# Moving attention work between the input projections, and a layer norm onto GpSimd, in a fused encoder block

## The reference, cut to what matters

```
h = rms_norm(x);  proj = h @ W_in                 # [q_down 256 | kv_down 128 | k_rope 32 | conv 1024 | gates 2048]
q = rms_norm(q_down) @ w_uq                       # 8 heads x 96
k_nope, v = split(rms_norm(kv_down) @ w_ukv)      # 8 heads x 64, 8 heads x 64
q, k = rope(rms_norm(q)), rope(rms_norm([k_nope, k_rope]))
attn = chunk_causal_attention(q, k, v)            # query tiles of 128; tile j sees keys 0 .. 128*(j+1)
u = depthwise_conv31(c_val * sigmoid(c_gate))     # 512 channels
u = silu(layer_norm(u));  gates = sigmoid(gate_logits + b)
x = x + W_out(gates_A * (attn @ w_o) + gates_B * (u @ w_conv_out))
x = x + moe(rms_norm(x))                          # routing and experts: not touched
```

## Time and profile before

| | us |
|---|---|
| median of 3 runs (lowest, highest) | 1282.66 (1280.54, 1284.18) |
| the profiled execution: its time | 1281.88 |
| its span, first to last instruction | 1279.8 |
| first matmul of the input units | 70.9 |
| first matmul of the branch units | 621.09 |
| first matmul with W_out | 710.35 |
| PE busy in the span | 1182.0 (92%) |
| DVE, ACT, POOL busy | 752.9, 468.1, 198.6 |

### The profile page before, as it was taken

One profiled execution on the slowest core, in us unless ns is written; L12 is line 12 of the kernel. 1 busy time (PEld: TensorE's weight loads), 2 busy tenths in 40 slices (PEclk: granted clock), 3 DMA queues, 4 the chain that ended last, 5 costly groups with the idle time before them and its releaser, 6 DMA issues.

```text
span 1279.8 us, 14988 instructions
## 1 busy us (share of the span) xinstructions
PE 1182.0 (92%) x5452; PEld 901.6 (70%) x5452; DVE 752.9 (59%) x992; ACT 468.1 (37%) x635; POOL 198.6 (16%) x243
## 2 busy tenths in 40 slices
PE   5999999999968999999899899949999989989996
PEld 5988888887645667767788788847666656666663
DVE  3338999993424455444466434476777556656673
ACT  4432111113443444444232211124555544554552
POOL 4010000000142232220000000011222221222221
PEclk8999999999969999999799899958999999999998
DMA  6011111110100000001320233494999999999980
GB/s 224 1 50 50 49 49 50 49 49 17 42 0 1 1 1 1 1 1 34 133 81 17 79 124 115 168 323 164 327 345 311 314 318 323 341 331 308 319 270 8
DMA packets 101542, 172.28 MB, mean 135 GB/s; under 512 B 11727, under 2 KB 45690, under 8 KB 101498
## 3 DMA queue, kind: packets, MB, share of 16 engines
q1 hardware_dynamic: 91002, 154.86, 35.6%
q0 software_dynamic: 10432, 16.81, 5.4%
q10 hardware_dynamic: 64, 0.02, 0.0%
HBM read 165.35 MB, written 27.26 MB: 151 GB/s over the span
## 4 chain that ended last, share of the span: by engine, by line
PE 68%; DMA 10%; SPq 5%; DVE 5%; issue 4%; ACT 4%; POOL 2%; ACTq 0%; DVEq 0%; POOLq 0%
PE pb L1223 14%; PE pb L1224 14%; PE pb L1225 14%; DMA wgu_raw<-in_w_e_up 9%; PE pb L1505 5%; PE pb L1363 4%; PE pb L1340 4%; SPq L418 2%; PE pb L1352 2%; PE pb L1272 2%; PE pb L1477 2%; PE pb L1282 1%; SPq L415 1%; SPq L414 1%; PE pb L1423 1%
## 5 line engine op out<-in xcount | busy, mean ns | idle before, releaser
L1165 DVE TENSOR_TENSOR wgu_lo<-wgu_raw,wgu_hi 128x2048 fp32r<-128x2048 f32 x72 | 164.5, 2286 | 60.0 <-ACT wgu_hi L772 59.9
L772 ACT ACTIVATE wgu_hi<-wgu_raw 128x2048 fp32r<-128x2048 f32 x72 | 137.1, 1907 | 53.0 <-DMA wgu_raw<-in_w_e_up 52.9
L873 DVE SCALAR_TENSOR_TENSOR cv<-up,dwc,cv 128x1024 f32<-128x1024 f32 x120 | 154.1, 1284 | 3.7
L1223 PE MATMUL pb<-hT_hi,ws_hi 128*128 128x512 f32 x384 | 151.7, 395 | 0.0
L1225 PE MATMUL pb<-hT_hi,ws_lo 128*128 128x512 f32 x384 | 149.5, 389 | 0.0
L1224 PE MATMUL pb<-hT_lo,ws_hi 128*128 128x512 f32 x384 | 149.5, 389 | 0.0
L1223 PE MATMUL pb<-wgu_hi,hgT_hi 128*128 128x512 f32 x288 | 128.6, 447 | 4.3 <-DVE hgT_lo L1172 4.3
L1505 PE MATMUL pb<-wed,midT 128*128 128x512 f32 x288 | 131.2, 599 | 0.5 <-DVE midT L1198 0.5
L1225 PE MATMUL pb<-wgu_hi,hgT_lo 128*128 128x512 f32 x288 | 114.3, 397 | 0.0
L1224 PE MATMUL pb<-wgu_lo,hgT_hi 128*128 128x512 f32 x288 | 113.9, 395 | 0.0
L1505 PEld LDWEIGHTS pb<-wed,midT 128*128 128x128 f32 x288 | 54.9, 191 | 56.4 <-issue 52.9
(11 more groups left out here) (281 smaller groups left out, 2028.8 us busy)
## 6 DMA issues: line engine op xcount, KB each, us to landing
wgu_raw<-in_w_e_gate SPq DMA_DIRECT2D x36, 1024.0 KB, 11.1
wgu_raw<-in_w_e_up SPq DMA_DIRECT2D x36, 1024.0 KB, 20.2
wed<-in_w_e_down SPq DMA_DIRECT2D x36, 1024.0 KB, 18.2
ws_raw<-in_w_in SPq DMA_DIRECT2D x24, 512.0 KB, 3.8
xs<-in_x SPq DMA_DIRECT2D x8, 512.0 KB, 8.6
...
```

Of the source, the lines that this page charges most:

```text
L772: a.activation(wgu_hi[q % 2][:, :, ks, :], wgu_raw[q % SLOTS][:, :, ks, :], ACT.Copy).then_inc(gu_hi, 1)
L873: i = v.scalar_tensor_tensor(out=cv[:, c, :], in0=src, scalar=w, in1=cv[:, c, :], op0=ALU.mult, op1=ALU.add)
L1165: v.tensor_tensor(wgu_lo[q % SLOTS][:, :, ks, :], wgu_raw[q % SLOTS][:, :, ks, :], wgu_hi[q % 2][:, :, ks, :].bitcast(F32), ALU.subtract). ...
L1223: t_.matmul(out, w(0), m(0), start=start, stop=False)
```

## The change

1. **Preparation moves up.** The nine pieces of all eight tiles are placed between the matmul steps of units 1 to 16, a tile to two units, at the steps `PREP_STEP` (32 steps to a pair). They use two PSUM banks in turn (6, 7). ACT now also copies qdT (as three activations, instead of one DVE instruction) and kT, and squares in PSUM; DVE only sums. SP stores q, k and v of each tile to DRAM and loads them back (`store_prep`, `load_q`, `load_k`, `load_v`), because their SBUF is not free yet. POOL's instructions for q and k stay the same but for one short one each.
2. **Heads of tiles 0 to 3 move up**, one to every three steps, from unit 17 to 23 (`HEAD0`, `PER_HEAD`, `MIXED` = 32). There ACT makes the copy of the transposed probabilities (`probs_early`), where DVE made it. Tiles 4 to 7 follow as a loop of their own.
3. **Taps**: 6 in a unit instead of 7, spread over the steps; DVE's part of each engine's stream follows the steps. The weights' lo half is made at step 6.
4. **Layer norm** goes into tiles 4 to 7: POOL adds the four channel groups, subtracts, squares, sums, multiplies, and splits the result into `aT`; PE needs 4 matmuls in place of 16; ACT copies the mean, takes the root (head 49) and runs Silu (heads 57, 59); DVE adds eps and takes the reciprocal in four parts (heads 50 to 53).
5. **Attention output** is transposed (`attn_T`) in heads 33 to 36, 42, 50 and 58, and split straight from PSUM by ACT and DVE (`attn_lo`). The last tile's follows the first half of branch unit 0.
6. **Gates** go through DRAM: one store a unit, 16 loads beside the branch units. The rotary angles and their sine come ahead of unit 0's eviction instead of after unit 1. `EARLY` is heads 44 and 45.

```diff
@@ -57,9 +57,10 @@
...
-TAPS_PER_UNIT = 7
+TAPS_PER_UNIT = 6
+STEPS = 2 * KD
...
-LN_UNIT = 20
+MIXED = 4 * 8
...
-        at_stage = {s: i for i, s in enumerate(order)}
...
+        PREP = ("qdT", "q0", "q1", "kv0", "kv1", "qT0", "qT1", "kT0", "kT1")
+        PREP_STEP = (0, 2, 5, 8, 11, 22, 24, 29, 31)
+        PREP_UNIT = 1
+        SUMS_LATE, LO_STEP = 4, 6
+        prep_at = {STEPS * PREP_UNIT + 2 * STEPS * t + g: (k, t) for t in range(NTILE) for k, g in zip(PREP, PREP_STEP)}
...
+        HEAD0, PER_HEAD = STEPS * 17 + 8, 3
+        scores_at = {HEAD0 - 10: 0, HEAD0 - 7: 1, HEAD0 + PER_HEAD * MIXED + 1: MIXED, HEAD0 + PER_HEAD * MIXED + 5: MIXED + 1}
+        scores_at.update({HEAD0 + PER_HEAD * n: n + 2 for n in range(MIXED - 2)})
+        probs_at = {HEAD0 + PER_HEAD * n: n for n in range(MIXED)}
+        pv_at = {HEAD0 + PER_HEAD * n + 2: n for n in range(MIXED)}
+        attn_T_at = {MIXED + 1: 0, MIXED + 2: 1, MIXED + 3: 2, MIXED + 4: 3, 42: 4, 50: 5, 58: 6}
...
+        MEAN_AT, VAR_AT, SQRT_AT, RECIP_AT, SILU_AT = (37, 38), (47, 48), 49, (50, 51, 52, 53), (57, 59)
...
+            def store_prep(u):
+                t, late = divmod(u - PREP_UNIT, 2)
+                if not 0 <= t < NTILE:
+                    return
+                if late:
+                    prep_freed(("qT0", t), ("qT1", t))
+                    sp.dma_start(qT_d[t], qst[0:QK, :]).then_inc(q_out, 16)
+                    prep_freed(("kT0", t), ("kT1", t))
+                    sp.dma_start(kT_d[t], kst[0:QK, :]).then_inc(k_out, 16)
+                else:
+                    prep_freed(("kv0", t), ("kv1", t))
+                    sp.dma_start(v_d[t], vst[:, :]).then_inc(v_out, 16)
+            def store_gate(u):
+                c = u - GLU_UNITS
+                if c >= 0:
+                    sp.wait_ge(u_ev, u + 1)
+                    sp.dma_start(gates_d[c], gst[:, c % 2, :]).then_inc(gate_out[c % 2], 16)
...
-            sp.wait_ge(u_mm, IN_UNITS - 1)
             sp.dma_start(wukv[:, :], w_ukv[0]).then_inc(ukv_in, 16)
-            sp.wait_ge(m_full, at_stage["kT1", NTILE - 1] + 1)
-            for c in range(OUT_UNITS):
+            for u in range(2, IN_UNITS):
+                store_gate(u - 4)
+                sp.wait_ge(u_hi, u - 1)
+                sp.wait_ge(u_lo, u - 1)
+                load_unit(u % 2, unit_col(u))
+                store_prep(u - 4)
+                if u == 16:
...
+            store_gate(IN_UNITS - 4)
+            load_q(4)
+            store_gate(IN_UNITS - 3)
+            load_branch(0)
+            store_gate(IN_UNITS - 2)
+            load_branch(1)
+            store_gate(IN_UNITS - 1)
+            for j in range(5, NTILE):
+                load_q(j)
...
+            load_branch(3)
+            sp.wait_ge(pv_ok, NTILE * HEADS)
+            for b in range(2):
+                sp.wait_ge(gate_out[b], 16 * GATE_UNITS // 2)
+            load_gates(0)
+            load_gates(1)
...
+            pool.wait_ge(conv_done, NC)
+            pool.wait_ge(u_mm, IN_UNITS)
+            link(g.tensor_tensor(lnm[:, :], cv[:, 0, :], cv[:, 1, :], ALU.add))
+            link(g.tensor_tensor(lnm[:, :], lnm[:, :], cv[:, 2, :], ALU.add))
+            g.tensor_tensor(lnm[:, :], lnm[:, :], cv[:, 3, :], ALU.add).then_inc(ln_sum, 1)
+            pool.wait_ge(ln_m, 2)
+            for c in range(NC):
+                link(g.tensor_tensor(cv[:, c, :], cv[:, c, :], lnr[:, :], ALU.subtract))
+                if c < 1:
+                    link(g.tensor_tensor(lnq[:, 0, :], cv[:, c, :], cv[:, c, :], ALU.mult))
+                else:
+                    link(g.tensor_tensor(lnq[:, 1, :], cv[:, c, :], cv[:, c, :], ALU.mult))
+                    i = g.tensor_tensor(lnq[:, 0, :], lnq[:, 0, :], lnq[:, 1, :], ALU.add)
+                    if c < NC - 1:
+                        link(i)
...
+            def prep(kind, t):
+                b, count = prep_slot(kind, t)
+                M = pb[:, 6 + b, :]
+                if kind == "qdT":
+                    act.wait_ge(prep_ps[b], count)
+                    for c in range(3):
+                        i = a.activation(qdT[:, c, :], M[:, c * P:(c + 1) * P], ACT.Copy, scale=vcol[:, V_GQ + c:V_GQ + c + 1])
+                    i.then_inc(prep_free[b], 1)
...
+            def probs_early(m):
+                w = (m // HEADS + 1) * P
+                act.wait_ge(pt_ok, m + 1)
+                if m >= 2:
+                    act.wait_ge(pv_ok, m - 1)
+                a.activation(pT[:, m % 2, 0:w], p_ps(m)[:, 0:w], ACT.Copy).then_inc(pt_d, 1)
...
             down_out(NTILE - 1)
+            act.wait_ge(sin_in, 1)
+            a.activation(sincos[:, :, :, :], sincos[:, :, :, :], ACT.Sin).then_inc(sin_ok, 1)
...
+                for s in range(STEPS):
+                    g = STEPS * (u + 1) + s
+                    if g in prep_at:
+                        prep(*prep_at[g])
+                    if g - 1 in probs_at:
+                        probs_early(probs_at[g - 1])
+                    if g - 2 in scores_at:
+                        exps(scores_at[g - 2])
...
+                    a.activation(lnr[:, f * 512:(f + 1) * 512], pb[:, 5, :], ACT.Copy).then_inc(ln_m, 1)
+                if n == SQRT_AT:
+                    act.wait_ge(ln_vc, 2)
+                    a.activation(lnr[:, :], lnr[:, :], ACT.Sqrt).then_inc(ln_sd, 1)
+                if n in SILU_AT:
+                    for c in (2 * SILU_AT.index(n), 2 * SILU_AT.index(n) + 1):
                         act.wait_ge(ln_y, c + 1)
                         a.activation(cv[:, c, :], cv[:, c, :], ACT.Silu, scale=vcol[:, V_GL + c:V_GL + c + 1],
                                      bias=vcol[:, V_BL + c:V_BL + c + 1]).then_inc(ln_u, 1)
...
+            dve.wait_ge(down_rs, 2)
...
+            rotary_angles()
+            link(v.tensor_scalar(ss3[:, 2, :], ss3[:, 2, :], 1.0 / QK, EPS, ALU.mult, ALU.add))
             taps_done = 0
...
+                for s in range(STEPS):
+                    for k in range(taps_done + fresh * s // STEPS, taps_done + fresh * (s + 1) // STEPS):
+                        tap(k)
+                    g = STEPS * (u + 1) + s
+                    if prep_at.get(g - SUMS_LATE, ("",))[0] in ("q0", "q1", "kv0", "kv1"):
+                        prep(*prep_at[g - SUMS_LATE])
+                    if s == LO_STEP and 2 <= u < IN_UNITS - 2:
+                        unit_lo(u + 2)
+                    if g - 1 in scores_at:
+                        rowmax(scores_at[g - 1])
+                    if g - 1 in pv_at and pv_at[g - 1] % HEADS == HEADS - 1:
+                        attn_norm(pv_at[g - 1])
+                taps_done += fresh
...
+            for m in range(MIXED, NTILE * HEADS):
+                probs_out(m)
                 if m + 2 < NTILE * HEADS:
                     rowmax(m + 2)
-                for k, t in slots(j, h, 1):
-                    misc(k, t)
+                if m - 1 in attn_T_at:
+                    attn_lo(attn_T_at[m - 1])
+                if m in VAR_AT:
...
+            def attn_T(t):
+                pe.wait_ge(on_ok, t + 1)
+                if t:
+                    pe.wait_ge(at_lo, t)
+                if t == 4:
+                    pe.wait_ge(ln_m, 2)
+                if t == 5:
+                    pe.wait_ge(ln_vc, 2)
+                for c in range(4):
+                    i = t_.transpose(pb[:, 5, c * P:(c + 1) * P], On[t % 4][:, c * P:(c + 1) * P], ident[:, :])
+                i.then_inc(ot_ps, 1)
...
+                for f in range(2):
+                    for k in range(KD):
+                        g = STEPS * u + f * KD + k
+                        if g in prep_at:
+                            prep(*prep_at[g])
+                        if g in probs_at:
+                            probs_T(probs_at[g])
+                        if g in scores_at:
+                            scores(scores_at[g])
+                        if g in pv_at:
+                            pv(pv_at[g])
+                        i = three(pb[:, 2 * b + 2 + f, :], lambda s: ws[s][:, b, k, :], lambda s: hT[s][:, k, f * 512:(f + 1) * 512], k == 0, k == KD - 1)
+                i.then_inc(u_mm, 1)
...
+            for n in range(MIXED, NTILE * HEADS):
                 probs_T(n)
...
                 if n + 2 < NTILE * HEADS:
                     scores(n + 2)
-                for k, t in slots(j, h, 1):
-                    misc(k, t)
+                if n in attn_T_at:
+                    attn_T(attn_T_at[n])
+                if n in MEAN_AT:
+                    ln_mean(MEAN_AT.index(n))
+                if n in VAR_AT:
+                    ln_square(VAR_AT.index(n))
                 pv(n)
-            misc("oT", NTILE - 1)
...
+            pe.wait_ge(u_lo, IN_UNITS + 1)
+            pe.wait_ge(cv_lo, NC)
+            branch(0, 1)
+            attn_T(NTILE - 1)
+            pe.wait_ge(at_lo, NTILE)
+            branch(0, 0).then_inc(u_mm, 1)
```

(45 more changed lines are left out.)

552 lines of the change are left out of this document (265 added, 287 removed).

## The result

The changed kernel takes 1291.7 us (median; 1287.56 to 1310.27), the kernel before 1282.18 in the same comparison: a ratio of 1.007 with a 95% interval of 1.0048 to 1.0091. It is slower, by 0.7%; I had forecast 1273, faster, by 0.7%. The profiled execution took 1287.56 us (span 1285.7), 5.7 more than that of before.

The account below looks back on a forecast made before the run. TensorE's own work was taken as 590.9 of 639.4 us, the rest waits and low clock. Work of 580.6 plus 49.1 lost gave 629.7, 9.7 less, hence 1273 us (range 1257 to 1296).

Parts of the forecast that it names:

- rival 2: Units 1 to 16: taps starve POOL, PE waits for q; 72 us more (1345), or 24 (1297); chance 0.22.
- `attn_lo` waits, 4 x 1.6 = 6.4: Heads 34 to 37: `attn_T`, then `ln_mean`, waits 1.6 us for `attn_lo` behind DVE's row maximum, four times.
- the clock at 1.0 from unit 2 on: Sign expected in the trace: PE's granted clock stays full from unit 2 onward.
- Pieces and early heads: Preparation pieces and first heads, moved between unit matmuls, cost PE the same there: pieces 6.54 a tile, heads 0.566 per key tile.
- Unit boundaries, 8.7: Heads in units 17 to 23: `pv` waits behind ACT's eviction and rounding at seven boundaries, 8.7 us (4 to 18).
- q0, 8 x 1.3: Units 1 to 16: PE waits 1.3 us a tile ahead of q0 for ACT's qdT copy, 10.4 in all.
- the start, 3.6 + 3: First q0: ACT's work queues behind the late sine, 3.6 us more wait, plus 3 (0 to 6) for low clock.
- GpSimd beside the taps, 7: Units 1 to 16: POOL and DVE's taps take turns, so PE waits about 0.9 us a tile, 7 in all.
- Silu and root, 5.5: Tiles 4 to 7: Silu with its table load and the root delay ACT's copies, 5.5 us (2 to 10).
- early splits, 3: Tiles 4 to 7: the two early weight splits cost 3 us.
- Rival 3: No change, 1282: ACT's bursts longer, both table loads of a boundary in the open, 9 us; chance 0.16.
- Transfers, gates, the end: Stores, loads and gates cost nothing (gates 0 to 5); `attn_T(7)` and its split at the end cost 1.5 us.

Follow-up runs that it names:

- experiment 1: Changed kernel with DVE's `attn_lo` put ahead of the row maximum in heads 32 to 63: 1275.8 us, ratio 0.996 to the kernel before.
- experiment 3: Changed kernel with pieces q0, q1, kv0 and kv1 placed two steps later, VectorE's sums keeping their steps: median 1296.6 us (1279.3 to 1303.3).
- 4: Changed kernel with VectorE making the rotary angles ahead of its wait for the down projections' reciprocal roots: median 1300.7 us (1285.9 to 1308.0).
- experiment 2: Changed kernel with the two early weight splits moved from heads 44 and 45 to 45 and 46: median 1303.8 us (1281.1 to 1311.8).
- 5: Kernel of experiment 1 with the first tile's `attn_lo` left behind the row maximum, so one wait of 1.6 us returns: median 1280.2 us.
- 6: Kernel of experiment 1 with the first two tiles' `attn_lo` left behind the row maximum, so two waits of 1.6 us return: median 1284.2 us.
- 10: Best version (five changes of order, 1255.66 us) with `attn_lo` put back behind the row maximum, so the four waits return: median 1268.98 us.

## Why the prediction was wrong

The bound was read rightly, and so were most waits and their places. The sign was wrong because the sum took waits at their own length: TensorE's clock behind them was priced once, at 3 us, and in the trace it cost 15.4 (nine stretches of 3.4 us at half clock between 72.8 and 626.9 us). That 1291.7 lies inside the stated range, 1257 to 1296, is luck: the upper part of that range belonged to rival 2, whose cause did not occur.

- **`attn_lo` waits, 4 x 1.6 = 6.4.** Wait and place exact (1.61, 1.61, 1.60, 1.60). *This is the term that failed*: with the clock behind them they cost 15.9 us (experiment 1, whose order leaves 0.9 of waits), 9.5 more than summed (13.2 in the changed kernel's own trace: 6.4 and four stretches of low clock, 6.8). I had priced the clock once, 3 us at the start, and wrote "the clock at 1.0 from unit 2 on", and that waits "of 3 us and more" would pull it down. Half that length did: in this trace, up to the branch units, each of the nine waits of 1.5 us and more was followed by a low stretch, and none of the shorter ones. The earlier trace rows hinted at it: a stretch of waits of 0.2 to 2.0 us at 0.66.
- **Pieces and early heads, "cost PE the same wherever they stand".** The period of a head of tile 0 is 3.00 us (340.90 less 337.90) against 2.76 (nine matmuls of 0.227, and 0.716). In tiles 1 to 3 the excess is 0.21, 0.19 and 0.18 (periods of 3.54, 4.08 and 4.64), so over the 32 heads the sum lacks 6.6 us. The pieces cost more there too: a pair of units takes 29.97 us (241.50 less 211.53) against 29.6, 2.8 for the eight. In the rows, the first unit matmul behind an inserted float32 piece pushes the next by 0.31 to 0.34 us instead of 0.23 (337.13 to 337.44, and 335.49 to 335.83):

```profile
337.13 0.47 PE L1347 MATMUL pb<-hT_hi,ws_hi 128*128 128x512 f32 x1
337.44 0.39 PE L1348 MATMUL pb<-hT_lo,ws_hi 128*128 128x512 f32 x1
337.67 0.39 PE L1349 MATMUL pb<-hT_hi,ws_lo 128*128 128x512 f32 x1
337.90 0.27 PE L1444 MATMUL pb<-ident,pr 128*128 128x128 f32 x1
```

- **Unit boundaries, 8.7.** Measured 1.10 + 1.73 + 0.42 + 1.00 = 4.3: overstated, and it offset part of the point above. Behind the 1.73 came one stretch of low clock (0.95 from 384 to 416 us), 1.7 us.
- **q0, 8 x 1.3, and the start, 3.6 + 3.** Right: 1.20 to 1.30 in seven tiles, and 4.74 at the first with one stretch of low clock behind it. Removing the first kind gave 9.0 us in the trace (experiment 3, where the low stretch at 384 us is missing too), the other 5.2 (4). The short ones, 30 us apart, cost their length and no more: the clock is 1.00 from 96 to 330 us.
- **GpSimd beside the taps, 7; rival 2.** In the changed kernel PE never waited for it, so the 7 us were not there; that stage came out 5.2 us below the sum. The engines do take turns, both ways. Groups of GpSimd's lines in the kernel after, from 64 to 330 us, then its timeline and VectorE's in one tile:

```profile
L601 POOL TENSOR_TENSOR qn<-qn,ssh 128x768 f32<-128x768 f32 x8 | 18.0, 2245 | 0.6
```
```profile
248.30 2.60 POOL L600 TENSOR_TENSOR ssh<-ssh,mhalf 128x8 f32<-128x8 f32 x1 [13.52 <-DVE ssh L1057]
250.98 2.36 POOL L601 TENSOR_TENSOR qn<-qn,ssh 128x768 f32<-128x768 f32 x1
```
```profile
250.73 3.69 DVE L995 SCALAR_TENSOR_TENSOR cv<-up,dwc,cv 128x1024 f32<-128x1024 f32 x2
```

  L601 is 2.25 us instead of 1.47, and two taps took 3.69 us instead of 2.57. Over 120 taps the mean is 1.395 against 1.284, 13 us of VectorE that PE did not wait for. The rule of the Trainium skill that I weighed (SBUF — State Buffer, Who interferes with whom) also says that the exclusion works both ways; the missing half, VectorE held by GpSimd, is now shown: 3.19 us for 1.23 in experiment 2's rows. GpSimd's chain for q took 10.4 us there (248.30 to 258.69), not the 12.1 that I had, and stood ready: rival 2 was far off.
- **Silu and root, 5.5; early splits, 3.** 1.54 + 2.13 + 0.43 = 4.1, and 3.25, each of the longer ones with a stretch of low clock behind it. The sizes hold roughly; most of the splits' 3.25 is GpSimd's hold on VectorE, which the sum does not name (1.07 without it).
- **Rival 3's table loads.** Seven sigmoid loads of 1.28 us, each over before its eviction began, as argued. Of the seven loads ahead of an exponential some did stand in the open, as at 345.25, ahead of the copy that ended PE's wait of 1.10 us; that was in the sum. The next instruction began right behind each load (384.20 behind the one at 382.90).
- **Transfers, gates, the end.** Hidden as said: 1.41 for `attn_T(7)`, where 1.5 was summed; the first branch unit waits for nothing else.

Put together: -5.2 for the units, +5.7 for the early heads, +12.6 for the late ones, +0.8 for the branch units, 13.9 us over the sum. By cause: +12.4 for the clock, +6.6 and +2.8 for heads and pieces between units, -4.4 for the boundaries, -7 for GpSimd; the remaining 3.5 are not traced. Not settled is why one execution leaves the low clock after 3.4 us and another stays in it for 68 with PE busy all the time; that such waits bring the clock down is shown by 1, 5, 6 and 10.
